# First merge block's sample rows placed one branch further in the second block

## The reference

```
u = rmsnorm(x, norm_g);  proj = u @ w_in          # split into the branch inputs and mg
z_a = (hs * silu(lg)) @ lru_wo                    # A: conv4, then the RG-LRU recurrence hs
z_b = (silu(sg) * sb * cy) @ sconv_wo             # B: short gated convolution cy
z_c = (o * silu(qg)) @ xa_wo                      # C: attention o into 256 memory tokens
g_a, g_b, g_c = split(sigmoid(mg), 3)
y = (g_a * z_a + g_b * z_b + g_c * z_c) @ w_out
return rmsnorm(x + y, final_norm_g), ...          # and the new states
```

## Time and profile before

| what | value |
|---|---|
| time before, median of 3 runs | 737.77 us (737.34 to 738.12) |
| the profiled execution, slowest core | 738.12 us, its span 736.6 us on core 2 |
| spans of the 8 cores | 734.2 to 736.6 us |
| mean granted TensorE clock of the cores | 0.990 to 0.997 of full |
| PE busy | 717.0 us, 97% of the span |
| DVE, ACT, POOL busy | 441.3, 338.1, 133.8 us |
| first, second, third merge block start on PE | 384.33, 414.74 (its first gate unit), 451.73 us |

### The profile page before, as it was taken

One profiled execution on the slowest core, in us unless ns is written; L12 is line 12 of the kernel. 1 busy time (PEld: TensorE's weight loads), 2 busy tenths in 40 slices (PEclk: granted clock), 3 DMA queues, 4 the chain that ended last, 5 costly groups with the idle time before them and its releaser, 6 DMA issues.

```text
span 736.6 us, 11607 instructions; the slowest of 8 cores (734.2 to 736.6 us)
## 1 busy us (share of the span) xinstructions
PE 717.0 (97%) x4378; PEld 357.6 (49%) x4378; DVE 441.3 (60%) x460; ACT 338.1 (46%) x434; POOL 133.8 (18%) x123
## 2 busy tenths in 40 slices
PE   5999999999999999999999999999999999999994
PEld 4884544444444444444444444444445454444542
DVE  3693141995967959869589465665643132325685
ACT  4591358768767777685871231211111111113343
POOL 4000000100010011000102334343434433322000
PEclk9999999999999999999999999999999999999998
DMA  8988242203112131030405108667564937577433
GB/s 194 263 242 125 42 109 37 49 2 58 30 16 42 29 58 30 1 57 1 73 1 99 45 13 147 145 171 174 156 108 55 148 59 108 87 207 260 172 146 143
DMA packets 24773, 71.84 MB, mean 98 GB/s; under 512 B 2464, under 2 KB 4784, under 8 KB 24592
## 3 DMA queue, kind: packets, MB, share of 16 engines
q0 software_dynamic: 10544, 36.05, 30.2%
q1 hardware_dynamic: 14032, 35.00, 14.8%
q10 hardware_dynamic: 144, 0.07, 0.0%
HBM read 93.27 MB, written 9.83 MB: 140 GB/s over the span
## 4 chain that ended last, share of the span: by engine, by line
PE 90%; DVE 4%; DMA 2%; issue 2%; ACT 1%; POOL 0%; DVEq 0%; ACTq 0%; POOLq 0%
PE PP L374 84%; PE PQ L374 5%; DMA R<-xp 2%; PE PQ L459 1%; DVE R L803 1%; DVE R L1015 0%; DVE R L1163 0%; DVE R L1167 0%; DVE R L810 0%; DVE R L1004 0%; DVE R L699 0%; DVE og L700 0%; POOL R L158 0%; ACT uT L1302 0%; DVE R L1299 0%
## 5 line engine op out<-in xcount | busy, mean ns | idle before, releaser
L374 PE MATMUL PP<-uT,R 128*128 128x512 bf16 (+2 forms) x2400 | 490.1, 360 | 1.4 <-DVE uT L471 0.8
L374 PEld LDWEIGHTS PP<-uT,R 128*128 128x128 bf16 x2400 | 226.4, 98 | 242.1 <-issue 2.7
L1158 ACT ACTIVATE R<-PP 128x1024 f32<-128x1024 f32 x48 | 49.2, 1025 | 198.0 <-PE PP L374 196.1
L1167 DVE SCALAR_TENSOR_TENSOR R<-R,PP 128x1024 f32<-128x1024 f32 x32 | 39.1, 1221 | 105.5 <-PE PP L374 96.2
L374 PE MATMUL PP<-R 128*128 128x512 bf16 (+1 forms) x408 | 81.1, 346 | 0.0
L1171 POOL TENSOR_TENSOR R<-R 128x1024 f32<-128x1024 f32 x16 | 42.7, 2668 | 110.5 <-DVE R L1167 101.0
L374 PEld LDWEIGHTS PP<-R 128*128 128x128 bf16 x408 | 34.6, 97 | 38.5
L1174 POOL TENSOR_TENSOR R<-R 128x1024 bf16<-128x1024 f32 x16 | 39.7, 2478 | 50.9 <-DVE R L1167 36.9
L716 DVE SCALAR_TENSOR_TENSOR R<-R,pT 128x1024 f32<-128x1024 f32 x36 | 45.7, 1282 | 2.9 <-DVE R L716 0.5
L374 PE MATMUL PP<-gA,R 128*128 128x512 bf16 x192 | 44.1, 379 | 0.0
L374 PE MATMUL PP<-gB,R 128*128 128x512 bf16 x192 | 44.1, 379 | 0.0
(11 more groups left out here) (174 smaller groups left out, 722.2 us busy)
## 6 DMA issues: line engine op xcount, KB each, us to landing
R<-wl POOLq DMA_DIRECT2D x32, 512.0 KB, 9.7
R<-ck SPq DMA_DIRECT2D x16, 512.0 KB, 6.0
y_p<-R SPq DMA_DIRECT2D x15, 512.0 KB, 2.6
R<-wl POOLq DMA_DIRECT2D x8, 768.0 KB, 10.0
uT<-xp SPq DMA_DIRECT2D x9, 512.0 KB, 8.4
R<-xp SPq DMA_DIRECT2D x8, 512.0 KB, 9.1
R<-xp POOLq DMA_DIRECT2D x8, 512.0 KB, 15.7
R<-cv POOLq DMA_DIRECT2D x16, 256.0 KB, 7.7
```

The source lines that it names most:

```text
L374: S.op("pe", lambda e, l=l, r=r, i=i: e.matmul(out_ap, l, r, start=(i == 0), stop=(i == n - 1)), reads=reads, writes=[wtok], inc=(last_inc ...
L1158: S.op("act", lambda e, pp=pp, th_=th_: e.activation(out=th_, in_=pp[:], func=AF.Tanh, scale=0.5), reads=[tk], writes=[tth])
L1167: S.op("dve", lambda e, th_=th_, zp=zp: e.scalar_tensor_tensor(out=th_, in0=th_, scalar=1.0, in1=zp, op0=ALU.add, op1=ALU.mult), reads=[tt ...
```

## The change

In the second block the first block's `merge_sample`, with the two `w_done` calls behind it, moves from after branch (h, xi) = (1, 0) to after branch (1, 1). No operation is added or removed.

```
--- before.py
+++ after.py
@@ -1213,7 +1213,7 @@
                     for xi in range(3):
                         merge_x(j, h, xi, *w_)
                         next(sgen, None)
-                        if late and (h, xi) == (1, 0):
+                        if late and (h, xi) == (1, 1):
                             j0, w0 = late.pop()
                             merge_sample(j0, *w0)
                             w_done(f"Mg{j0}")
```

## The result

The changed kernel takes 747.02 us (median of 4 runs, 746.90 to 748.02) against 737.91 us before (4 runs): the ratio is 1.013, with a 95% interval of 1.0116 to 1.0144, so 1.3% or 9.1 us slower. The prediction was 745.7 us in a range of 743.2 to 749.3.

A forecast was written before the change was run, and what follows sets the result against it. PE bounds the kernel, with 90% of the chain that ended last. Mo0's landing put the third block's product unit 6.93 us late, 7.93 with the clock's loss in the gate unit: 737.77 + 7.93 = 745.7 us, range 743.2 to 749.3.

The forecast's parts named there:

- PE's gain: Second block: the late sample rows no longer wait for gB, so PE reaches the third block 0.64 us earlier.
- POOL's loss: POOL's queue: both loads wait behind branch (1, 1)'s product and addition, Mg0 issued at 448.06 us, 8.6 us later than before.
- The landing: Third block's loads: Mg0 lands 9.9 us and Mo0 13.5 us after issue, leaving PE idle 6.87 us.
- core 2's later pair: The fourth block's pair of loads in the profile before, 9.9 and 13.5 us, taken as the landing of the changed pair.
- The clock: Third block's first gate unit: PE returns from the wait at 1.2 GHz for 3.4 us and loses 1.7 us.
- The sum: Third block's first product unit starts 7.93 us late; added to the 737.77 us median, 745.7 us.
- The forecast's own narrower range: Whole kernel: 744.5 to 747.5 us, from a landing of 9 to 10.5 us and a clock loss of 0.7 to 3.4.
- The hidden load: Rival at the third block: both loads still arrive in time, only the removed wait counts, 737.1 us; chance 0.04.
- The clock holds: Rival at the third block: clock holds or recovers at once, only the loads count, 6.93 us, 744.7 us; chance 0.22.
- The loads land later still: Rival at the third block: loads share DMA engines with the next pair and key load, 10.9 us late, 748.7; chance 0.19.
- the pair in the earlier trace: A later pair before the change, issued behind two SP loads, 12.9 and 14.8 us; used as the landing's slow bound.

The follow-up runs named there:

- e5: Kernel before, but the sample matmuls from gA and gB and Mo0's load move between branch (1, 1)'s gate and product units; 737.72 us against 738.37, ratio 0.9992.
- e1: Kernel before, with only the third block's two weight loads moved behind branch (1, 1), sample rows left in place; 748.48 us, ratio 1.0134.
- e2: Changed kernel, with the sample rows and two loads emitted ahead of POOL's addition of branch (1, 1); 743.50 us, ratio 1.0067.
- e9: Changed kernel, but 12 sample matmuls and Mo0's load back behind branch (1, 0), plus 110 constant matmuls keeping PE busy; 746.21 us, ratio 1.0115.
- e3: Changed kernel, with 110 matmuls on constants keeping PE busy while it waits for the load; 748.35 us, ratio 1.0127.
- e4: Changed kernel, with the fourth block's pair of loads issued later, in the third block behind branch (0, 1); 748.04 us, ratio 1.0130.
- e6: Changed kernel, with both 110 constant matmuls keeping PE busy and the fourth block's pair of loads issued later; 746.48 us, ratio 1.0113.
- e7: The changed kernel itself, run again; 747.88 us, ratio 1.0132 against the kernel before.
- e8: Changed kernel, but the 12 sample matmuls from gA and gB and Mo0's load go back behind branch (1, 0); 748.23 us, ratio 1.0142.

## Why the prediction was right, and which terms were off

- **PE's gain.** 0.64 us forecast. From the start of branch (1, 1) to the end of the second block I had 13.91 us; the trace has 451.37 - 437.46 = 13.91. e5 measured the 0.64 us by itself. Right.
- **POOL's loss.** The pair was forecast 10.88 us after branch (1, 1) starts, behind product and addition; it was 10.84. e1 and e2 show both halves of it. Right.
- **The landing.** One of two terms that were mis-sized. I took core 2's later pair, 9.9 and 13.5 us; core 4 had 10.7 and 15.6. For `Mo0` that was the fault of taking one core: over the 8 cores of the kernel before, the second tile of that later pair landed in 12.7 to 15.2 us. For `Mg0`, which set the end, it was not: the first tile took 8.1 to 9.9 us there, so core 2 was already at the slow end, and in the changed kernel `Mg0` took 8.5 to 11.4. Why it landed later is open.
- **The clock.** The other mis-sized term. It fell, as forecast, but PE had 0.50 for over 5 us of the gate unit instead of 3.4, and the unit lost 2.65 us on core 4 (6.1 against 3.45) instead of 1.7. The unit ended last, as forecast: at 465.19, 0.74 us after `Mo0` had landed (448.85 + 15.6 = 464.45); I had 1.0 us for the same thing (463.11 against 462.11). So holding the clock alone would have given back 0.74 us on that core, as `Mo0` lay behind it. e9 shows 1.8 us where nothing hides it; e3's gain can't be told from none.
- **The sum.** 7.93 us forecast. On core 4 the stretch grew by 27.73 - 17.99 = 9.74 us, so 1.8 us more. In the forecast's own terms 0.8 of these are `Mg0`'s landing (10.74 against 9.9) and 1.0 the clock. That core also began the stretch about 1.0 us later than before (437.46 against 436.48), and the median time rose by 9.1 us. The range held both errors. The forecast's own narrower range, 744.5 to 747.5, is not what its two ends give together, about 744 to 748.
- **The rivals.** The hidden load didn't happen. "The clock holds" was wrong in its premise, though on the slowest core the time that `Mo0` alone would have set wasn't far from the measured one. "The loads land later still" was nearest in size, but e4 and e6 don't show its cause, and `Mg0` didn't land as late as it says: 8.5 to 11.4 us, where the first tile of the pair in the earlier trace rows took 11.4 to 12.9 over the 8 cores of the kernel before.

## What to carry to other kernels

When an operation moves, follow what stands behind it in the program: here the cheap part moved harmlessly, and two load issues, tied to it by a freed slot, slid behind an addition in another engine's queue and used up a margin of 2.6 us. If a buffer's last reader has to wait, split it so that each load is released by the reader it needs (e5: 0.64 us of the stretch). And when two bounds end close together (a landing and a slowed unit, here 0.2 to 2.1 us apart), price the change by the later one on the slowest core: taking that one away alone gives back only the gap to the other.

## What the runs showed of the hardware that was not expected

The landing time of the same 512 KB load, at the same place in the program, ranged from 12.3 to 15.2 us over the cores of one run (e7) and up to 16.7 us in another (e3), and the runs don't show what sets the difference between cores. Alone in the queue, with no `Mg0` just ahead, the same load took 5.9 to 8.0 us (e8 and e9). And TensorE's clock fell on one core in or just after a wait of 2.0 us and stayed on another through 3.1 us (e2), so after waits of this length the unit behind can take some 2 us longer on one core and no longer on the next.
